# One core, attention over 16 blocks of queries: the turn of a block's first head moved behind the next step's maximum, and the three heads interleaved by 32 columns so that one instruction makes a block's high part

## The reference, cut to what matters

```python
def attend_block(args):          # n: one of 4 blocks of 128 queries
    n, qn = args
    kw = lax.dynamic_slice_in_dim(kp, n * BLOCK, BLOCK + 2 * WINDOW, axis=1)
    vw = lax.dynamic_slice_in_dim(vp, n * BLOCK, BLOCK + 2 * WINDOW, axis=1)
    s_win = jnp.einsum('bqkgd,bjkd->bkgqj', qn, kw).astype(jnp.float32) * scale
    s_ctx = jnp.einsum('bqkgd,bjkd->bkgqj', qn, k_ctx).astype(jnp.float32) * scale
    ...
    s_win = jnp.where(valid, s_win, -jnp.inf)
    logits = jnp.concatenate([sink_logits(sink, s_win.shape[:-1]), s_ctx, s_win], axis=-1)
    p = jax.nn.softmax(logits, axis=-1)
    ...
    return (jnp.einsum('bkgqj,bjkd->bqkgd', p_ctx, v_ctx)
            + jnp.einsum('bkgqj,bjkd->bqkgd', p_win, vw))
```

## Time and profile before

| | |
|---|---|
| median of 3 runs | 1455.17 us (1454.86 to 1456.14) |
| the profiled execution | 1457.66 us, span 1455.8 us (1.9 us lie around the span) |
| TensorE busy | 1385.8 us (95%) |
| VectorE, ScalarE, GpSimd busy | 860.9 (59%), 515.5 (35%), 137.6 us (9%) |
| mean granted TensorE clock | 0.988 of 2.4 GHz |
| attention stage | 383 to 700 us |

### The profile page before, as it was taken

One profiled execution on the slowest core, in us unless ns is written; L12 is line 12 of the kernel. 1 busy time (PEld: TensorE's weight loads), 2 busy tenths in 40 slices (PEclk: granted clock), 3 DMA queues, 4 the chain that ended last, 5 costly groups with the idle time before them and its releaser, 6 DMA issues.

```text
span 1455.8 us, 19083 instructions
## 1 busy us (share of the span) xinstructions
PE 1385.8 (95%) x7258; PEld 1151.5 (79%) x7258; DVE 860.9 (59%) x1327; ACT 515.5 (35%) x798; POOL 137.6 (9%) x273
## 2 busy tenths in 40 slices
PE   5999999999979899777899999999999999999998
PEld 3788888888868777666788888888888888887888
DVE  6544656466667585665565577757767333475434
ACT  5323422254545443443222233112255222323332
POOL 0001111011122212122011101001100000010000
PEclk9999999999999999899999999999999999999999
DMA  9996667566544445345766666446633333366423
GB/s 386 408 395 214 200 204 251 171 201 212 146 110 117 117 109 124 94 118 128 262 205 198 200 183 195 149 118 199 200 92 101 102 96 93 102 186 190 125 87 116
DMA packets 79170, 251.20 MB, mean 173 GB/s; under 512 B 13792, under 2 KB 20976, under 8 KB 77680
## 3 DMA queue, kind: packets, MB, share of 16 engines
q1 hardware_dynamic: 53376, 164.48, 36.3%
q0 software_dynamic: 24032, 80.47, 18.2%
q10 hardware_dynamic: 1680, 5.10, 1.1%
HBM read 231.63 MB, written 4.23 MB: 162 GB/s over the span
## 4 chain that ended last, share of the span: by engine, by line
PE 76%; DVE 8%; DMA 5%; SPq 4%; issue 3%; ACT 2%; POOL 0%; DVEq 0%; ACTq 0%
PE ps L1596 76%; SPq L447 3%; DMA modchunk<-cond_row 2%; DVE pt_lo L1304 1%; DMA kvmem<-in_ctxT 1%; DVE cond_row L1291 1%; DVE w_lo L988 1%; DMA cond_row<-in_mod 1%; ACT pt_hi L769 1%; DVE kvmem L1281 1%; DVE tmp L1114 1%; DVE tmp L1281 1%; DMA kvmem<-inverses 1%; ACT w_hi L557 1%; DVE main L1312 1%
## 5 line engine op out<-in xcount | busy, mean ns | idle before, releaser
L1596 PE MATMUL ps<-h_hi,w_hi 128*128 128x512 f32 x1592 | 625.8, 393 | 5.8 <-DVE w_lo L988 4.0
L1596 PE MATMUL ps<-h_lo,w_hi 128*128 128x512 f32 x1592 | 622.6, 391 | 0.0
L1596 PE MATMUL ps<-h_hi,w_lo 128*128 128x512 f32 x1592 | 621.9, 391 | 0.0
L988 DVE TENSOR_TENSOR w_lo<-raw,w_hi 128x1024 fp32r<-128x1024 f32 x206 | 252.0, 1223 | 385.5 <-ACT w_hi L557 385.0
L557 ACT CAST w_hi<-raw 128x1024 fp32r<-128x1024 f32 x206 | 215.9, 1048 | 620.0 <-PE ps L1596 620.0
L1596 PEld LDWEIGHTS ps<-h_hi,w_hi 128*128 128x128 f32 x1592 | 302.0, 190 | 70.4 <-issue 8.1
L1596 PEld LDWEIGHTS ps<-h_hi,w_lo 128*128 128x128 f32 x1592 | 301.6, 189 | 63.6
L1596 PEld LDWEIGHTS ps<-h_lo,w_hi 128*128 128x128 f32 x1592 | 301.7, 190 | 59.4
L994 DVE CUSTOM_DVE_ANT_0 modchunk<-modchunk,cond_row 128x1024 f32<-128x1024 f32 x128 | 154.6, 1220 | 19.7 <-DMA modchunk<-in_modb 19.5
L496 POOL DMA_DIRECT2D modchunk<-in_modb x128 | 67.7, 529 | 835.0 <-DVE modacc L994 809.1
L531 POOL DMA_DIRECT2D modchunk<-cond_row x128 | 62.6, 497 | 245.6 <-DVE cond_row L1291 241.8
(11 more groups left out here) (230 smaller groups left out, 1381.9 us busy)
## 6 DMA issues: line engine op xcount, KB each, us to landing
raw<-in_weights SPq DMA_DIRECT2D x208, 512.0 KB, 3.6
modchunk<-in_modb POOLq DMA_DIRECT2D x128, 512.0 KB, 4.7
raw<-in_mod SPq DMA_DIRECT2D x32, 512.0 KB, 9.0
modchunk<-in_mod SPq DMA_DIRECT2D x16, 512.0 KB, 7.5
cond_row<-in_mod SPq DMA_DIRECT2D x16, 512.0 KB, 8.9
main<-in_xT SPq DMA_DIRECT2D x4, 1024.0 KB, 8.6
main<-in_xT ACTq DMA_DIRECT2D x4, 1024.0 KB, 7.5
out<-pooled SPq DMA_DIRECT2D x16, 256.0 KB, 2.5
```

What stands on the lines that cost most here:

```text
L988: nc.vector.tensor_tensor(low, src, high.bitcast(F32), ALU.subtract).then_inc(lo_ready, 1)
L1596: return nc.tensor.matmul(out, lhsT, rhs, start=start, stop=stop, skip_group_check=True)
```

## The change

`turn_blocks` of a block's first head moves from the end of slot 3n to the next slot, behind `maximum(3n + 1)`. The layout of `cond_row` and `modchunk` changes: within a quadrant the columns were (head, tile, 32), they become (tile, head, 32). The turned probabilities of a tile then lie as (quadrant, head, 32) in one run of 384 columns of `pt_hi` and `pt_lo`, instead of (head, 128). One instruction for a block (1536 or 1920 columns) takes the place of three (512 or 640 each) on ScalarE and on VectorE, and it raises the semaphore by 3. `turned_blocks` writes runs of 32 columns with a stride of 96 between the tiles, where it wrote one run of tiles x 32. `block_out` reads its columns in the new order. The moves, their sizes and their order are the same.

```diff
--- before.py
+++ after.py
@@ -307,24 +307,21 @@
         last_squares = [tmp[:, 0, 0:SEQ], tmp[:, 1, 0:SEQ], scratch[:], ubuf[:, 1, 0:SEQ]]
         eye = ubuf[:, 3, 0:P]
 
-        def turned_tiles(k, dst):
-
-            tiles, j = key_tiles(k), k % GQA
-            return dst[:, 0:tiles, j * P:(j + 1) * P].rearrange("p t (a c) -> p t a c", c=QUADRANT)
-
         def block_runs(n, mem):
 
             return mem[:, 0:GQA * key_tiles(n * GQA) * P].rearrange("p (a x) -> p a x", a=4)
 
         def turned_blocks(k):
 
-            run = key_tiles(k) * QUADRANT
-            return block_runs(k // GQA, cond_row)[:, :, k % GQA * run:(k % GQA + 1) * run].rearrange("p a (t c) -> p a t c", c=QUADRANT)
-
-        def landed_tiles(k):
-
-            run = key_tiles(k) * QUADRANT
-            return block_runs(k // GQA, chunk_flat)[:, :, k % GQA * run:(k % GQA + 1) * run].rearrange("p a (t c) -> p t a c", c=QUADRANT)
+            return block_runs(k // GQA, cond_row).rearrange("p a (t j c) -> p a t j c", j=GQA, c=QUADRANT)[:, :, :, k % GQA]
+
+        def whole_turned(n, dst):
+
+            return dst[:, 0:key_tiles(n * GQA)].rearrange("p t (a x) -> p t a x", a=4)
+
+        def whole_landed(n):
+
+            return block_runs(n, chunk_flat).rearrange("p a (t x) -> p t a x", x=GQA * QUADRANT)
 
         def block_source(n, a, j):
 
@@ -759,14 +756,13 @@
                                      bias=stat[:, 1, k % 2:k % 2 + 1], scale=-1.0,
                                      accum_out=rowsum[:, b % 2, k % GQA:k % GQA + 1]).then_inc(exp_done, 1)
 
-            def turned_hi(i, k):
-
-                g = i * STEPS + k
-                if k % GQA == 0:
-                    moves_landed(act, g // GQA)
-                    if g:
-                        act.wait_ge(pv_done, g // GQA)
-                nc.scalar.copy(turned_tiles(k, pt_hi), landed_tiles(k)).then_inc(pt_hi_ready, 1)
+            def turned_hi(i, n):
+
+                b = i * BLOCKS + n
+                moves_landed(act, b)
+                if b:
+                    act.wait_ge(pv_done, b)
+                nc.scalar.copy(whole_turned(n, pt_hi), whole_landed(n)).then_inc(pt_hi_ready, GQA)
 
             def last_swap(i, k):
 
@@ -799,8 +795,7 @@
                     if k in UNIT_SLOTS:
                         hi(i + G_Z, UNIT_SLOTS.index(k) + 2)
                     if k in HIGH_SLOTS:
-                        for j in range(GQA):
-                            turned_hi(i, HIGH_SLOTS.index(k) * GQA + j)
+                        turned_hi(i, HIGH_SLOTS.index(k))
                     if i < 2:
                         last_swap(i, k)
                     if last and k in PAIR_SLOTS:
@@ -1298,20 +1293,21 @@
                     dve.wait_ge(inverse_written[b % 2], 16 * (b // 2))
                 nc.vector.reciprocal(inverse[:, b % 2], rowsum[:, b % 2]).then_inc(inverse_ready, 1)
 
-            def turned_lo(i, k):
-
-                dve.wait_ge(pt_hi_ready, i * STEPS + (k + 1))
-                nc.vector.tensor_tensor(turned_tiles(k, pt_lo), landed_tiles(k), turned_tiles(k, pt_hi).bitcast(F32),
-                                        ALU.subtract).then_inc(pt_ready, 1)
+            def turned_lo(i, n):
+
+                dve.wait_ge(pt_hi_ready, (i * BLOCKS + n + 1) * GQA)
+                nc.vector.tensor_tensor(whole_turned(n, pt_lo), whole_landed(n), whole_turned(n, pt_hi).bitcast(F32),
+                                        ALU.subtract).then_inc(pt_ready, GQA)
 
             def block_out(i, n):
 
                 b = i * BLOCKS + n
                 dve.wait_ge(pv_done, b + 1)
                 dve.wait_ge(inverse_landed, 16 * (b + 1))
-                nc.vector.tensor_tensor(main[:, i * GQA + FG:(i + 1) * GQA + FG, n * P:(n + 1) * P],
-                                        ps[:, 7, P:512].rearrange("p (j q) -> p j q", j=GQA),
-                                        inverse_row.rearrange("p (q j) -> p j q", j=GQA), ALU.mult).then_inc(y_done, 1)
+                y = main[:, i * GQA + FG:(i + 1) * GQA + FG, n * P:(n + 1) * P]
+                nc.vector.tensor_tensor(y.rearrange("p j (a c) -> p j a c", c=QUADRANT),
+                                        ps[:, 7, P:512].rearrange("p (a j c) -> p j a c", a=4, c=QUADRANT),
+                                        inverse_row.rearrange("p (a c j) -> p j a c", c=QUADRANT, j=GQA), ALU.mult).then_inc(y_done, 1)
 
             def attention(i):
 
@@ -1319,6 +1315,8 @@
                 for k in range(SLOTS):
                     if k < STEPS and (k or first):
                         maximum(i, k)
+                    if 1 <= k < STEPS and k % GQA == 1 and (k > 1 or first):
+                        turn_blocks(i, k - 1)
                     if k in QUERY_SLOTS:
                         n = QUERY_SLOTS.index(k) + 1
                         piece(i * PIECES + (5 + n), q_lo[:, n % 2],
@@ -1326,8 +1324,7 @@
                     if k == NEXT_SCORES and not last:
                         maximum(i + 1, 0)
                     if k in LOW_SLOTS:
-                        for j in range(GQA):
-                            turned_lo(i, LOW_SLOTS.index(k) * GQA + j)
+                        turned_lo(i, LOW_SLOTS.index(k))
                     if k == 1:
                         piece(i * PIECES + 4, v_lo[:, 0:BLOCKS], values[:, :, i * P:(i + 1) * P], v_hi[:, 0:BLOCKS])
                         piece(i * PIECES + 5, v_lo[:, BLOCKS:], values_c[:, :, i * P:(i + 1) * P], v_hi[:, BLOCKS:])
@@ -1337,8 +1334,6 @@
                         invert_sums(i, k // GQA)
                     if k in UNIT_SLOTS:
                         lo(i + G_Z, UNIT_SLOTS.index(k) + 2)
-                    if k < STEPS and k % GQA == 0 and (k or first):
-                        turn_blocks(i, k)
                     if k in BLOCK_SLOTS:
                         block_out(i, BLOCK_SLOTS.index(k))
                     if last and k in PAIR_SLOTS:
```

## The result

The changed kernel takes **1431.14 us** (median of 4 runs, 1429.32 to 1431.89); the kernel before took 1455.66 us beside it (median of 4, 1454.86 to 1456.98). The ratio is 0.9829, with a 95% interval of 0.9812 to 0.9846: 24.5 us, 1.7%, faster. The profiled execution took 1431.89 us at a span of 1430.0 us, 25.8 us less than that of before.

A forecast was written before the change was run, and what follows sets the result against it. TensorE was taken to wait for maxima queued behind a turn that waits for the previous block's moves. Savings of 15.3 + 3.5 + 4.4 + 6.4 = 29.6 us from 1455.2 gave 1426 us, range 1411 to 1443.

The forecast's parts named there:

- The forecast case: Whole kernel: the summed gain holds, 1426 us, between 1420 and 1432; chance 0.57.
- The turn moved: a period of 14.5 us: Iterations 0 and 1: 14.5 us from one block's moves to the next in place of 17.05; 15.3 us over 6 periods.
- Iteration 2 and iteration 3, first two periods: Attention, first two periods of each: 30.9 to 27.4 us saves 3.5, and 35.0 to 30.6 saves 4.4.
- The third periods of iterations 2 and 3: Block 2's late landings: 4.5 of TensorE's 7.7 us wait stays, for `w_lo`; 3.2 us saved each, 6.4 together.
- Merging, 0.34 us a block: Three instructions become one: 0.12 us a block for `pt_lo`, 0.22 for the high part; alone at most 4 us.
- The turn's new pattern at 0: VectorE's turns writing 32-column runs with gaps: no extra time taken, upper bound 4 us over 36 turns.
- Rival (D): VectorE's turns: gapped writes cost; 0.8 us more a turn cancels the gain, 1.2 more gives 1469 us; chance 0.07.
- Rival (A): Attention stage: TensorE's last waits vanish too and the clock stays up, saving 43 us, to 1412; chance 0.15.
- The stretch of 486.10 to 503.10 us that it named as a sign: One block's period in iteration 1: mean clock 1.00, against 0.95 with all waits, cited for rival (A).
- Rival (B): Each of 12 periods: `w_lo` or q's low part takes half of what the maximum gave, 15 us, 1440; chance 0.17.
- Rival (C): Attention periods: the wait for a maximum only moves by a slot, leaving 4 us of merging, 1451; chance 0.04.

The follow-up runs named there:

- Experiment 1: The kernel before with only the first head's turn moved behind the next maximum: 1431.77 us; the changed kernel with that turn put back: 1454.73 us.
- Experiment 2: The changed kernel with ScalarE's high part of q made a slot earlier, ahead of the sink that waits for the turn: 1426.02 us, ratio 0.9797.
- the last kernel of experiment 6: The changed kernel with q's high part earlier, the reload and one weight load later, and rotations moved behind the block's last turn: 1411.96 us, ratio 0.9681.

## Why the prediction was right, and where it was off

The forecast case held: 1426 us against 1431, with the range of 1411 to 1443 around it. 29.6 us were forecast, 24.5 measured.

- *The turn moved: a period of 14.5 us.* Right. The first two iterations gave 44.1 and 44.5 us for three periods, against 43.5. Experiment 1 shows that this edit alone brings 24.4 us. From the landing to the next moves 8.1 us were worked out; the last period of iteration 1 has 506.93 - 498.80 = 8.1. But it is another chain than the one told in two periods of three: in slots 4 and 10 the turn, `w_hi` behind the sink (0.6), `w_lo` (1.2), the rotations (1.4) and the maximum lie on VectorE ahead of `pt_lo`. The prediction called the `w_lo` "needed later" and didn't name the rotations. That the two chains are about equally long is why the number came out. Experiment 2 and the last kernel of experiment 6 show both: q early shortens only the middle periods of iterations 0 and 1, the rotations only the others. So the number is in part luck. In the middle period of iteration 1 one more step differs: the turn goes 7.0 us after the first issue, right behind a maximum (483.20) that itself waited 1.68 us for its scores. The prediction had it ahead of the landing.
- *Iteration 2 and iteration 3, first two periods:* 4.2 for 3.5 and 3.7 for 4.4; right in sum. The 3.5 doesn't follow from its own terms: two periods at TensorE's 13.9 are 27.8, not 27.4, and would give 3.1. And 13.9 was no floor: the two took 13.4 and 13.2. It was the busy time of a stretch, which counts the modelled end of each product ahead of a wait.
- *The third periods of iterations 2 and 3, "3.2 each, 6.4":* **the term that was mis-sized**; 2.0 and 1.2 were measured, and this is 3.2 of the 4.4 us that are missing. `w_lo` was to be ready 15.1 us after the last turn and needed at 10.6. It was ready at 15.9 (572.6 less 556.7): the 12.5 us to the landing came out, but they count from GpSimd's first issue, which is 0.3 us behind the last turn's end, and `w_lo` waits 0.61 us for a `w_hi` that stands on ScalarE behind the sink of the moved turn, a step that was left out. It was needed at 10.8. So 5.14 of 7.71 us stayed in iteration 2, and 5.64 of 6.91 in iteration 3. There the prediction itself had read that the wait was 0.8 shorter and still took 3.2; and its "12.5 us" wasn't what that place had. Before, the moves landed there 11.7 us after the first issue (657.54 to 669.20), now 12.7 (633.43 to 646.09). Why 1.0 us later is open. That the two waits would be for `w_lo`, and of 4 to 5 us, was right.
- *Merging, 0.34 us a block:* the lengths were right: 2.15 and 1.80 us against 2.17 and 1.76. On ScalarE 0.18 us a block was saved, not 0.22 (1.98 - 1.80), on VectorE 0.14 (2.29 - 2.15), not 0.12. "Alone at most 4 us" held; it was 1.7, and nothing measurable beside the moved turn. The Trainium skill's some 150 cycles of set-up an instruction ("VectorE: DVE Perf Modes", the side-by-side table) would have given 0.31 us on VectorE, by estimate. The measured 0.14 decides against it for instructions that follow one another: three of 0.82 us took 2.29 in a row.
- *The turn's new pattern at 0:* right, 0.84 us for 640 columns, and 0.71 for 512. Rival (D) needed 0.8 us more a turn and had none.
- *Rival (A), all waits go:* not here. 24.6 us of TensorE's waits are left in the stage. The stretch of 486.10 to 503.10 us that it named as a sign, at a clock of 1.00, holds waits of 1.63 and 1.43 us: short waits left the clock up there, the two long ones didn't. The last version of experiment 6, at 1412, is where (A) had put it, but has four more edits.
- *Rival (B), the next wait takes over:* in part. The wait for `w_lo` took 10.8 us of what the maximum gave, in the two places that were named, and nowhere else.
- *Rival (C):* no. TensorE waits for no maximum any more, of any head.

## What to carry to other kernels

On an engine with a fixed order, a wait costs what is queued behind it: putting the waiting instruction behind the one that others need is worth more than making either shorter (24 us against 1.7). When the wait is for a transfer that lands late, moving independent work past it passed nearly all of the wait to the next item that depends on it; find what the transfer shares the DMA engines with, and move that (6.2 and 6.7 us for one transfer put off, each). A wait that long also costs what TensorE loses behind it at the lower clock, here 2 to 2.4 us. Size what remains of a wait from the chain of the transfer through every engine to the instruction that needs it, the steps on the second engine included. And when a kernel gets faster, look whether the gain lies where the edit was.

## What the runs showed of the hardware that was not expected

- GpSimd issues the 8 moves of a block 0.49 us apart, but in block 2 of iteration 2 it pauses 3.1 to 3.3 us between the fifth and the sixth, in all twelve kernels of this study, whatever time of the span that is (553 to 581 us). It goes with the place in the program, then, not with the time; its cause isn't in the profile ("issue").
- Behind that pause the last three moves land 1.5 us after the end of their issuing, 5.3 us after it beside a 512 KB load; a block's 16 moves take 6.3 us from GpSimd's first issue and 12.7 beside a 1 MB reload that another engine issued.
- Behind a wait of 5.14 us TensorE's granted clock was 0.50 for 5.3 us, behind one of 5.64 us for 3.6 us; behind one of 1.28 us in the same place it was 1.00.
- A turn that writes runs of 32 columns with gaps takes as long as one that writes them in one piece: 0.84 and 0.71 us for 640 and 512 columns, both ways.
